# A decoder layer with 64 routed experts: the expert weights loaded in parts of 256 and 512 KB, with at most two parts on the way

## What is computed

```python
def body(acc, blk):                      # one block: 128 (token, expert) pairs of one expert e
    toks, bw, e = blk
    xb = hp[toks]                        # gather 128 rows of h
    yb = (jax.nn.silu(xb @ w_gate[e]) * (xb @ w_up[e])) @ w_down[e]
    return acc.at[toks].add(yb.astype(f32) * bw[:, None]), None
...
h = _layernorm(ALPHA * h + ffn, ln2_g[l], ln2_b[l])     # ffn = routed sum + shared expert
```

## Time and profile before

| | before |
|---|---|
| median of 3 runs | 2588.36 us |
| profiled execution: time, span | 2585.82 us, 2584.0 us |
| TensorE matmul busy | 2344.0 us, 91% |
| VectorE busy | 1835.5 us, 71% |
| ScalarE busy | 1229.0 us, 48% |
| GpSimd busy | 1270.5 us, 49% |
| SyncE's DMA queue | 336.64 MB, 38.9% of the engines' time |
| GpSimd's DMA queue | 186.90 MB, 29.8% of the engines' time |
| mean granted TensorE clock | 0.955 |

### The profile page before, as it was taken

The page is one execution under the profiler, slowest core; times in us unless marked ns, Lnnn a source line. Parts: engine busy times, 40 slices in busy tenths (PEclk is TensorE's granted clock), DMA queues, the critical chain, the costliest instruction groups (busy, mean ns, idle before and its releaser), DMA issues. The chain is left out here.

```text
span 2584.0 us, 47703 instructions
## 1 busy us (share of the span) xinstructions
PE 2344.0 (91%) x10684; PEld 1865.7 (72%) x10686; DVE 1835.5 (71%) x2304; ACT 1229.0 (48%) x1781; POOL 1270.5 (49%) x1005
## 2 busy tenths in 40 slices
PE   8899999899989698998999999989899998999986
PEld 6677777688867477777777777777777776777765
DVE  6676767768778676776776767677776667767658
ACT  3525353523327355454555455555554445555444
POOL 0010101011110567776667777677776667767637
PEclk9999999899989899999999999999999999899999
DMA  6232322564554688888988788988887778898873
GB/s 245 76 140 97 115 90 90 156 211 154 192 177 151 216 237 228 226 234 239 268 224 234 212 244 234 263 232 258 243 241 223 216 206 254 254 255 212 217 216 138
DMA packets 277263, 524.37 MB, mean 203 GB/s; under 512 B 32304, under 2 KB 191696, under 8 KB 273104
## 3 DMA queue, kind: packets, MB, share of 16 engines
q1 hardware_dynamic: 219952, 336.64, 38.9%
q0 software_dynamic: 56640, 186.90, 29.8%
q10 hardware_dynamic: 608, 0.02, 0.0%
HBM read 386.61 MB, written 136.87 MB: 203 GB/s over the span
## 5 line engine op out<-in xcount | busy, mean ns | idle before, releaser
L1636 POOL DMA_INDIRECT xg<-htab,gi x664 | 829.6, 1249 | 238.9 <-issue 190.9
L2541 PE MATMUL psG<-gu_split,xT_hi 128*128 x2624 | 643.7, 399 | 4.0 <-ACT xT_hi L2355 2.0
L2541 PEld LDWEIGHTS psG<-gu_split,xT_hi 128*128 128x128 f32 x2624 | 511.1, 195 | 116.0 <-issue 4.7
L2435 DVE STREAM_TRANSPOSE xF<-xg 128x1024 f32<-128x1024 f32 x165 | 352.9, 2139 | 267.3 <-DMA xg<-htab,gi 259.8
L2342 POOL DMA_INDIRECT acc<-y,si x162 | 301.2, 1859 | 251.1 <-DMA acc<-y,si 191.0
L2551 PE MATMUL psG<-gu_split,xT_lo 128*128 x1304 | 344.3, 406 | 18.4 <-issue 17.5
L2587 PE MATMUL psY<-d_hi,HT_lo 128*128 x648 | 223.7, 429 | 111.1 <-DVE HT_lo L2505 88.9
L2445 DVE TENSOR_TENSOR gu_split<-raw_gu,gu_split (+1 forms) x127 | 284.0, 2279 | 5.0 <-issue 5.0
L2551 PEld LDWEIGHTS psG<-gu_split,xT_lo 128*128 128x128 f32 x1304 | 234.7, 189 | 69.1 <-issue 26.2
L2369 ACT ACTIVATE gu_split<-raw_gu x126 | 234.3, 1908 | 24.1 <-issue 22.4
L2587 PEld LDWEIGHTS psY<-d_hi,HT_lo 128*128 128x128 f32 x648 | 124.9, 203 | 162.2 <-issue 139.8
(11 more groups left out here) (391 smaller groups left out, 3560.7 us busy)
## 6 DMA issues: line engine op xcount, KB each, us to landing
raw_gu<-in_w_gate_dram SPq DMA_DIRECT2D x64, 1024.0 KB
raw_gu<-in_w_up_dram SPq DMA_DIRECT2D x64, 1024.0 KB
raw_d<-in_w_down_dram SPq DMA_DIRECT2D x64, 1024.0 KB
wring<-split_d SPq DMA_DIRECT2D x24, 1024.0 KB, 4.8
xg<-htab,gi POOLq DMA_INDIRECT x664
split_d<-wring POOLq DMA_DIRECT2D x8, 1024.0 KB, 4.2
raw_d<-mixed SPq DMA_DIRECT2D x16, 512.0 KB, 4.4
xt<-in_x_dram SPq DMA_DIRECT2D x16, 512.0 KB, 4.8
```

Source lines behind the costliest of these rows:

```text
L1636: nc.gpsimd.indirect_dma_start(out=to[:, g, 0:PIECE], out_offset=None, in_=htab.rearrange("r a w -> (r a) w"), in_offset=bass.IndirectOffs ...
L2435: nc.vector.transpose(xF[slot][:, 0:KC, :].rearrange("p c (g j) -> p c g j", g=QUADS), xg[slot][:, :, 0:D // QUADS].rearrange("p g (i c) - ...
L2541: nc.tensor.matmul(psG[slot][:], xT_hi[slot][:, c, :], right[:, bass.ds(w, 1), c, :].rearrange("p a n -> p (a n)"), start=(n == 0 and c == ...
```

## The change

The 1 MB loads of the routed experts are cut: gate and up into 4 parts of 256 KB (two of the eight chunks `k` each), down into 2 parts of 512 KB. Each matrix gets two semaphores, for even and odd parts. In the routed stage a part is issued only when the part two ahead of it, in the order gate, up, down, next gate, has landed. The waits for the buffer (`gulo_s`, `dlo_s`) are kept. `prefetch_first` and `prefetch_second` issue the parts one behind the other without that wait. Whoever waits for a matrix waits for both of its semaphores. The shared expert is still loaded in DMAs of 1 MB.

```diff
+GU_PARTS, D_PARTS = 4, 2
...
+def weight_parts(w, dst, down, by_run=False):
+
+    n = D_PARTS if down else GU_PARTS
+    each = (FE // P if down else KC) // n
+    rows = w.rearrange("a (p k) n -> p (a k) n" if by_run and not down else "a (k p) n -> p (a k) n", p=P)
+    for q in range(n):
+        at = slice(q * each, (q + 1) * each)
+        yield dst[:, at, :], rows[:, at, :]
...
+                    ahead = [(down_in, D_PARTS, e - 1, q) for q in range(D_PARTS - 2, D_PARTS)]
                     for w, sm, dst in ((w_gate, gate_in, wgu[:, s, :, 0:FE]), (w_up, up_in, wgu[:, s, :, FE:]),
                                        (w_down, down_in, wd[:, s])):
...
-                        sp.wait_ge(sm, e * 16)
-                        carry_wait(sp, passed)
-                        rows = "a (k p) n -> p (a k) n" if sm is down_in else "a (p k) n -> p (a k) n"
-                        sp.dma_start(dst, w[0, bass.ds(e, 1)].rearrange(rows, p=P)).then_inc(sm, 16)
+                        n = D_PARTS if sm is down_in else GU_PARTS
+                        for q, (to, rows) in enumerate(weight_parts(w[0, bass.ds(e, 1)], dst, sm is down_in, by_run=True)):
+                            last, of, load, part = ahead.pop(0)
+                            sp.wait_ge(last[q % 2], load * (16 * of // 2) + 16 * (part // 2 + 1))
+                            carry_wait(sp, passed)
+                            sp.dma_start(to, rows).then_inc(sm[q % 2], 16)
+                            ahead.append((sm, n, e, q))
...
-                act.wait_ge(gate_in, e * 16 + 16)
-                act.wait_ge(up_in, e * 16 + 16)
+                for p in range(2):
+                    act.wait_ge(gate_in[p], (e + 1) * (16 * GU_PARTS // 2))
+                    act.wait_ge(up_in[p], (e + 1) * (16 * GU_PARTS // 2))
```

More of the change, by code:

```diff
@@ L1871, in _ @@
                     act.wait_ge(disp_s, TILES)
-                    act.wait_ge(loaded[0], 16)
-                    act.wait_ge(loaded[1], 16)
+                    for w in range(2):
+                        for p in range(2):
+                            act.wait_ge(loaded[w][p], 16 * GU_PARTS // 2)
                     for at in halves:
@@ L2147, in _, with load_expert @@
                     down(n)
[L2150 to L2154, removed]
+def weight_parts(w, dst, down, by_run=False):
[5 more added lines that the diff above has]
+        yield dst[:, at, :], rows[:, at, :]
+def load_expert(eng, w_gate, w_up, w_down, expert, slot, wgu, wd, loaded, in_parts=False):
+    gate, up = wgu[:, slot, :, 0:FE], wgu[:, slot, :, FE:]
+    for w, sm, dst in zip((w_gate, w_up, w_down), loaded, (gate, up, wd[:, slot])):
+        if in_parts:
+            for q, (to, rows) in enumerate(weight_parts(w[0, expert:expert + 1], dst, w is w_down, by_run=True)):
+                eng.dma_start(to, rows).then_inc(sm[q % 2], 16)
+        else:
+            eng.dma_start(dst, w[0, expert].rearrange("(k p) n -> p k n", p=P)).then_inc(sm, 16)
 def experts(nc, passed, w_gate, w_up, w_down, ident, htab, acc, table, n_turns, idx, pidx, tails_s, xg, gi, gi_s, x_in, acc_out, gu, guhi_s, gulo_s, wgu, wd, loaded, y, si, added,
@@ L2317, in _ @@
                 prefetch(sp)
-            for sm in (gate_in, up_in, down_in):
-                sp.wait_ge(sm, 16 * EXPERTS)
+            for sm, parts_ in ((gate_in, GU_PARTS), (up_in, GU_PARTS), (down_in, D_PARTS)):
+                for p in range(2):
+                    sp.wait_ge(sm[p], 16 * parts_ // 2 * EXPERTS)
         @block.gpsimd
@@ L2372, in _ @@
             block0, block1 = entries(act, 0, 2)
-            act.wait_ge(down_in, 16)
+            for p in range(2):
+                act.wait_ge(down_in[p], 16 * D_PARTS // 2)
             pieces = list(parts(0, 1))
@@ L2389, in split_down @@
                 e = entry.next()
-                act.wait_ge(down_in, e * 16 + 16)
+                for p in range(2):
+                    act.wait_ge(down_in[p], (e + 1) * (16 * D_PARTS // 2))
                 if before is not None:
@@ L3054, in decoder_layer @@
               w_out, raw_gu, raw_d, wo_hi, wo_lo, shared, early)
-        loaded = [ctx.enter_context(nc.semaphore(n)) for n in ("gate_in", "up_in", "down_in")]
+        loaded = [[ctx.enter_context(nc.semaphore(f"{n}{p}")) for p in range(2)] for n in ("gate_in", "up_in", "down_in")]
         shared_in = ctx.enter_context(nc.semaphore("shared_in"))
@@ L3083, in prefetch_first @@
         def prefetch_first(eng):
-            load_expert(eng, w_gate, w_up, w_down, 0, 0, raw_gu, raw_d, loaded, by_run=True)
+            load_expert(eng, w_gate, w_up, w_down, 0, 0, raw_gu, raw_d, loaded, in_parts=True)
         def prefetch_second(eng):
-            for sm in loaded:
-                eng.wait_ge(sm, 16)
-            load_expert(eng, w_gate, w_up, w_down, 1, 1, raw_gu, raw_d, loaded, by_run=True)
+            for sm, n in zip(loaded, (GU_PARTS, GU_PARTS, D_PARTS)):
+                for p in range(2):
+                    eng.wait_ge(sm[p], 16 * n // 2)
+            load_expert(eng, w_gate, w_up, w_down, 1, 1, raw_gu, raw_d, loaded, in_parts=True)
         place_in = ctx.enter_context(nc.semaphore("place_in"))
```

## The result

| | before | after |
|---|---|---|
| median | 2587.05 us (7 runs) | 2597.59 us (7 runs) |
| ratio to before | 1 | 1.0052, 95% interval 1.0032 to 1.0073 |
| profiled execution, span | 2584.0 us | 2598.8 us |

The forecast was 2530 us, faster. The time lies inside the range of 2465 to 2630 us, on the other side of no change, and outside the forecast's own range of 2485 to 2565 us.

The account below looks back on a forecast made before the run. Bound: TensorE's work plus gaps from gathers and scatters held behind weight loads. Gains 53 + 7 + 30 less costs 20 and 12 make 58 us off 2585.8, 2528, plus 2 for the median: 2530 us, range 2465 to 2630.

Parts of the forecast that it names:

- The reading of the bound: Routed stage: weight bursts hold gathers and scatters some 4 us, so TensorE stalls, 88.9 us of it on HT_lo.
- (a): Gathers and scatters behind weights: two parts in flight shorten the hold, saving 53 us at HT_lo and 7 elsewhere.
- the signs named: Waits should fall: VectorE for gathers below 170 us, GpSimd for scatters below 100, TensorE for HT_lo to about 40.
- Rival 2: Weights' queue: its length does not matter to gathers, so no gain there; 2588 us; chance 12%.
- (b): TensorE's clock in the routed stage: fewer stalls mean less time at the lower clock, 30 us gained, bounds 0 and 64.
- 198 us of loss: Routed stage ceiling on any gain: 133.6 us without a matmul plus 64 us lost to the lower clock.
- (d): SyncE's weight parts wait on each other: chain 23 us per expert against a need of 24.4, charged 12 us.
- rival 1: SyncE's wait for the part two ahead: the chain becomes the bound; at 26 us per expert 2684 us; chance 23%.
- its cover: Gate load issue to first read, 27.6 us: backlog can reach 10 us before ScalarE waits for weights.
- (e): Extra instructions: SyncE issues 10 DMAs per expert instead of 3, ScalarE waits on more semaphores; 0, at most 5 us.
- (c): Routed blocks: weights in the queue for more of the time delay most gathers and scatters a little; 20 us lost.
- The sum: Whole kernel: gains of 53, 7 and 30 us less costs of 20 and 12 make 58 us less.

Follow-up runs that it names:

- three in flight: Changed kernel with three parts in flight instead of two and one semaphore per part, against the kernel before: 2512.53 us against 2583.22 us, ratio 0.9722.
- small scatter: Changed kernel, two parts in flight, with the scatter-add cut from 512 KB to 32 KB per block, against the kernel before: 2421.03 us, ratio 0.9413.

## Why the prediction was wrong, point by point

*The reading of the bound* was right. Gathers and scatters held behind 2 MB of weights cause most of TensorE's stalls: take the weights away and 122 us go, and TensorE's wait for HT_lo falls from 88.9 to 16.4 us.

*(a), the freed gathers*, was right in its mechanism: the signs named (below 170, below 100, about 40 us) all came. TensorE's wait for HT_lo fell by 52.1 us where 53 were forecast, but the nearness is in part luck. In the changed kernel TensorE waits 86.1 us for HT_hi, which comes ahead of HT_lo, and such a wait can hide one for HT_lo. With the weights on time, in three in flight, HT_lo fell by 24.7 us, and by 44.3 with the wait of no named releaser beside it. What two in flight would have given with the weights on time, no run shows. Rival 2 is out, by the 80.9% and 45.6% against 4.6% of the engines in the same place.

*(b), the clock*, was right in its reasoning and did not come, since new stalls took the place of the old: 0.96 before and after. Where the stalls do go, with three in flight, it is 0.99. That is 2% of 1535 us at the lower level, 31 us, against 129 us before, worth 49 us by the prediction's way of counting. But that way counts as lost also the lower clock in the gaps, where no matmul runs. The matmuls themselves became 29.5 us shorter; 30 were forecast. For the same reason the 198 us of loss were too high a ceiling.

*(d), the weights' chain*, is the step that failed, and in it the term for contention. The chain was put at 23 us per expert: 18.1 by its own latency and 5 of contention. It took 24.9. The small scatter shows where: with the scatters nearly gone the chain takes 18.5, gathers still in it, so the first term was large enough, and the contention, taken as half of the 11.2 us that the other queue holds the engines, is at least 6.4. A pair of 256 KB rounds was priced at 2 x 3.4 = 6.8 us; it took 7.4 and 7.2 beside the gathers alone, and 9.3 and 9.8 with the scatters. The estimate of 13.6 us that the prediction worked out from the fit in the Trainium skill (DMA: Bandwidth & Descriptors, section Anatomy of one DMA) is well below the 18.5 us; the page gives that fit for DMAs that GpSimd issues, and these are SyncE's. Two microseconds per expert decided the sign, because the need was 24.4 and, once the gathers were freed, would have been 23.4 (three in flight: gate loads from 871.7 to 2301.6 us, 1429.9/61). The prediction saw a margin of 1.4 us against ends at 11.6 and 32, and still took the chain as short enough, with a charge of 12 us and a chance of 23% for rival 1.

The second fault of that step is its cover. The 27.6 us between a load and its first use was set against single short experts. A chain longer than the mean need uses up any cover: at 24.9 against 23.4 us, the 10 us of backlog that were allowed are gone within seven experts. Cover evens out a spread and not a mean. ScalarE's wait for weights was to stay under 20 us if (d) held; it was 144.4 us, and 11.8 with three in flight.

*Rival 1* was the right mechanism, at the point it named (24.4 us), though it priced 25 us per expert at +37 us; the span is 14.8 us longer. Its price took every expert's excess as time and left out that the last expert's load now comes nearer to the end of the stage: its first gate part starts at 2395.0, 100 us before 2495, against 2361.8 to 2480, 118 us.

*(e)* was put at 0 to 5 us; parts without a limit cost about 11 us. That these are the instructions that (e) counted is not shown: in that run the waits for gathers, scatters and HT_lo are longer as well. *(c)*, the thin stream of weights all through, was not separated by any run.

*The sum* of 58 us, 2528, is near what three in flight gives (71 us), made up there of 43.4 us of gaps and 29.5 of matmul time in the profiled runs. The gain was there to be had, but not with the chain that came with two.

## What to carry to other kernels

A prefetch that nobody waits for can still set the time, by standing in the DMA engines ahead of a small transfer that somebody does wait for; look at the share of each queue in the few microseconds behind a large issue. Limit the bytes in flight, but first set the length of the paced chain, measured beside the other queue's traffic, against the mean time per unit of work and not against the slack of one load. Here, counted in parts of gate and up, 512 KB in flight was too few (1.005), 768 KB right (0.972), 1 MB nearly so (0.982), and at 1.5 MB the gain is gone (1.002): try the neighbours before a limit is kept or dropped.

## What the runs showed that was not expected

The hold is not proportional to the bytes ahead. With six parts in flight VectorE's wait for gathers (320.0 us) is above that with the full 2 MB queued at once (259.8), while from three to four parts nothing moves (155.3 and 153.1). Part of the first difference can be the choice of the run, 2591.13 us against a median of 2576.38; the step from four to six is far larger than that. What in the engines makes the step between 1 and 1.5 MB was not found.

The Trainium skill (DMA: Bandwidth & Descriptors, section Queues, rings and completion order) has each engine go round its queues by packets; taken alone, that would make the depth of one queue indifferent to the other. Rows 8 and the runs from three to six in flight speak against it as the whole rule: with the depth of SyncE's queue alone changed, VectorE's wait for gathers went from 155.3 to 320.0 us. Whether the gathers' packets of rows 8 already stood in their queue while the weights' went through, no row shows.

The scatter-adds are dear although TensorE never waits for one directly: 480 KB less per block took 2576.47 to 2454.99 us, 121 us, as much as all the weights (122 us). And 18 DMAs per expert instead of 10 cost nothing measurable, so the number of DMAs was not the price of small parts here.
